# Ranks of queries and keys transposed by VectorE in 32x32 blocks and by transfers through device memory, with the queries' units amid the pool projection's

## The chip, the cores and the metric

One core of one Trainium2 chip runs the whole kernel in one launch. The metric is the device time of a launch in microseconds (us), the median of several executions. Nothing else runs on the chip.

## The reference, cut to what matters

Two layers of a decoder trunk on 256 tokens of width 1024, all in fp32. The mixer of a layer projects the normed tokens into several parts, among them the ranks `c_q` (384 wide) and `c_kv` (256 wide), each of which is normed and projected again; the pool branch has its own 512 columns `u_pool`:

```python
z = rms_norm(x, norm_pre) @ w_in
c_q, c_kv, k_r, u_conv, u_pool, gate_logits = jnp.split(z, split_at, axis=-1)
q = (rms_norm(c_q, q_norm) @ w_uq).reshape(B, S, N_HEADS, 96)      # 64 + 32 rotary
c_kv_n = rms_norm(c_kv, kv_norm)
k_nope, v = c_kv_n @ w_uk, c_kv_n @ w_uv
...                                  # causal attention, convolution, pooling, gates
x = x + rms_norm(merged @ w_mix_o, norm_post)
x = x + rms_norm((silu(h @ w_gate) * (h @ w_up)) @ w_down, ffn_norm_post)
```

## The kernel before, in words

The weights stream through the core in 135 units per layer, each 128 rows of up to 1024 fp32 numbers. A ring of 5 slots holds them. For every unit SyncE loads `raw` (line 398), ScalarE copies it into `w_hi`, rounded (`hi`, line 863), VectorE stores the rest as `w_lo` (`lo`, lines 1184 and 1188), and TensorE makes three products of high and low parts (`mm3`, lines 460 to 462). A slot is loaded again when `lo` of the unit five before is done (line 397); `hi` also waits until TensorE has used the slot; TensorE waits for `lo` (`unit_ready`). So each engine has one queue in program order, and the order of the work is written out by hand: the lists of `his`, `los` and `taps` in the scalar and vector blocks say after which unit something else stands.

The stage around the change, as it is before, in units of a layer: gate and value of the convolution (0 to 7), `CQ` (8 to 11, the rank of the queries), `CKV` (12 to 15, the rank of keys and values and the rotary key), `Q` (16 to 18, the queries out of their rank), `POOL` (19 to 22), `K` (23), `V` (24), and the 24 units of the gates (25 to 48), after each of which `attention(i)` puts a step of attention on TensorE's queue: scores, transposes of the probabilities, weighted values (lines 713 to 774).

A product needs the activation with its channels on the partitions. The ranks leave TensorE with tokens on the partitions, ScalarE scales them into `cq` (lines 955 and 968), and TensorE turns them with an identity (`transposes`, line 534): six for `CQ` before the third unit of `CKV`, four for `CKV` after `Q`. ScalarE copies the turned blocks out of PSUM as the high part (`hi_T`, line 897), VectorE stores the low part (`lo_T`, line 1216).

VectorE has one more task here: the convolution, 124 `taps` a layer (line 1263, 128x256 each), which are strewn between the `lo`s so that the last is done in the gates' stage; and it rotates and turns the heads of queries and keys with 32x32 transposes (`turn_heads`, line 1323), whose blocks are put in place by transfers on the POOL queue (line 1641) and on SyncE's (`move_keys`, line 360). In the gates' stage its loop (lines 1408 to 1427) has for gate unit i: `maxima` of the scores, `invert`, `divide`, `lo` of the unit four on, four taps. ScalarE's `exponentials` wait for `maxima`, TensorE's transposes of the probabilities (line 534, `tp<-const,qk`) for `exponentials`.

The hidden layer of the FFN is already turned in the other way: VectorE transposes 32x32 blocks (line 1502), SyncE moves the blocks from partition group to partition group inside SBUF (`place`, line 425, four issues at a time between loads), ScalarE and VectorE make high and low parts of what has landed (lines 1104 and 1509).

Of the kernel before, what the change touches and what calls it, by code (L numbers as in the profile page):

```python
# [14 lines left out]
P = 128  # L15
# [22 lines left out]
(U_G, U_A, U_CQ, U_CKV, U_Q, U_POOL, U_K, U_V, U_GATE, U_POOLO, U_ATTNO, U_CONVO, U_MIX, U_FFN,  # L38
 U_LAST, U_DOWN, UNITS) = (0, 4, 8, 12, 16, 19, 23, 24, 25, 49, 53, 57, 61, 69, 109, 113, 135)
# [19 lines left out]
def lo_count(g):  # L59
# [33 lines left out]
TP = (["X0", "X1", "X2", "X3", "HC0", "HC1", "CQ0", "CQ1", "CKV0", "CKV1",  # L93
# [44 lines left out]
def unit_scales(u):  # L138

    if U_Q <= u < U_POOL:  # L140
        return [(0, HEADS * QK, C_QN + u - U_Q)]
    if u in (U_K, U_V):
        return [(0, 512, C_KVN), (512, WU, C_KVN + 1)]
    if U_POOLO <= u < U_ATTNO:
        i = (u - U_POOLO) % 2
        return [(0, 512, C_PS + 2 * i), (512, WU, C_PS + 2 * i + 1)]
    return None


def build(nc, W, pool_w, par_d, const_d, gain_d, x_d, xc_d, pos_d, out_d):  # L150
    with ExitStack() as ctx:
# [59 lines left out]
        placed_q = [qk_flat[:, 512 * i:512 * (i + 1)] for i in range(QUADS - 1)] + [gates[:, 1, 512:1024]]  # L211
        rope_a, rope_b = hc[:, 0, :], hc[:, 1, :]
# [66 lines left out]
        k_nope = sem("k_nope")  # L279
        q_turned = sem("q_turned")  # L280
# [22 lines left out]
        stored = sem("stored")  # L303

# [48 lines left out]
        def move_keys(eng, l, part):  # L353

            for h in range(2):
                eng.wait_ge(misc_full[h], l * 2 + 1)
            for i in range(HEAD_MOVES // 2 * part, HEAD_MOVES // 2 * (part + 1)):
                c, q = divmod(i, QUADS)
                eng.wait_ge(k_turned, l * (QK // BLK) + c + 1)
                eng.dma_start(u_hc[BLK * c:BLK * (c + 1), q // 2, q % 2, :], turned_k[c][BLK * q:BLK * (q + 1), :]  # L360
                              ).then_inc(k_in[part], 16)

# [21 lines left out]
        def _(sp):  # L384
# [41 lines left out]

            for l in range(LAYERS):
                for u in range(0 if l else 1, UNITS):
# [10 lines left out]
                    if u == U_POOL:  # L439
                        load_pool_weights(l)  # L440
                    if u == U_GATE + 5:
                        move_keys(sp, l, 1)
# [14 lines left out]
        def _(pe):  # L457
# [23 lines left out]
            for l in range(LAYERS):  # L481
# [25 lines left out]
                def col_group(u0, n, per, width, pair, use, srcT, kt0=0, beside=None, after=None, mid=None, begun=0):  # L507

                    for i in range(begun, n):
# [143 lines left out]
                def cq_transposes(i):  # L653
                    if i == 2:
                        for t in range(TOK):
                            acc_freed(pe, l, t, "CQ")
                            transposes(TPN["CQ0"] + t, [(cq[:, t, c * P:(c + 1) * P], P) for c in range(3)])

                col_group(U_CKV, 4, 2, CKV_W, 1, "CKV", XT, beside=cq_transposes)

                for i in range(3):
                    unit_ready(U_Q + i)
                    for t in range(TOK):
                        if i == 0:
                            tp_emptied(pe, l, TPN["CQ0"] + t)
                            bank_free(t, "Q")
                            misc_wait(t, M_Q)
                        mm = tok_mm(base + U_Q + i, t, [i], 384, [acc[:, t, 0:384], misc[:, t, 0:384]], HT, 0, 2)
                        if t == 1:
                            mm.then_inc(unit_used, 1)  # L670
                        elif i == 2:
                            mm.then_inc(full[0], 1)
                for t in range(TOK):
                    acc_freed(pe, l, 2 + t, "CKV")
                    transposes(TPN["CKV0"] + t, [(cq[:, t, c * P:(c + 1) * P], P) for c in range(3, 5)])

                col_group(U_POOL, 4, 2, 512, 1, "POOL", XT)

                for t in range(TOK):
                    tp_emptied(pe, l, TPN["CKV0"] + t)  # L680
# [166 lines left out]
        def _(act):  # L847
# [3 lines left out]
            for l in range(LAYERS):  # L851
# [111 lines left out]
                for t in range(TOK):  # L963
                    hi_T(f"CQ{t}", hT_hi[:, H_CQ:H_CQ + 3, tokens(t)])
# [5 lines left out]
                his(20, 22)  # L970
# [3 lines left out]
                for t in range(TOK):  # L974
                    hi_T(f"CKV{t}", hT_hi[:, H_CKV:H_CKV + 2, tokens(t)])
# [7 lines left out]
                his(22, 23)  # L983
# [8 lines left out]
                his(23, 26)  # L992
# [156 lines left out]
        def _(dve):  # L1149
# [23 lines left out]
            for l in range(LAYERS):  # L1173
# [122 lines left out]
                for u in range(13, 16):  # L1296
                    lo(u)
                    taps(2)
                los(16, 17)
                for t in range(TOK):  # L1300
                    lo_T(f"CQ{t}", hT_lo[:, H_CQ:H_CQ + 3, tokens(t)], hT_hi[:, H_CQ:H_CQ + 3, tokens(t)])
                los(17, 18)
                taps(1)
                for u in range(18, 22):
                    lo(u)
                    taps(2)
                for t in range(TOK):
                    lo_T(f"CKV{t}", hT_lo[:, H_CKV:H_CKV + 2, tokens(t)], hT_hi[:, H_CKV:H_CKV + 2, tokens(t)])
                taps(3)
                los(22, 23)  # L1310
                taps(2)
# [14 lines left out]
                los(23, 24)  # L1326
                dve.wait_ge(q_roped, l + 1)
                turn_heads(q_sb, turned_q, q_turned)
                los(24, 25)
# [356 lines left out]
def unit_width(u):  # L1686
# [3 lines left out]
    if U_CKV <= u < U_Q:  # L1690
        return 2 * CKV_W
    if U_Q <= u < U_POOL:
# [4 lines left out]
def weight_stream(a):  # L1697
# [16 lines left out]
    put(U_POOL, pool, 2)  # L1714
# [73 lines left out]
```

## Time and profile before

| | us |
|---|---|
| median of 3 runs | 786.53 (786.52 to 786.84) |
| profiled execution, its own time | 786.49 |
| its span in the profile | 784.7 |
| PE busy | 776.2 (99%) |
| DVE busy | 573.3 (73%) |
| ACT busy | 421.8 (54%) |
| mean rate of the DMA engines | 197 GB/s |

The span runs from the first to the last recorded instruction; the execution's own time has 1.8 us more around it. PE is TensorE, DVE is VectorE, ACT is ScalarE, SP is SyncE; PEld is the loading of TensorE's stationary operand. The granted clock of TensorE has 9 or more tenths in every slice of the page, and its mean over the profiled execution is 0.998. The first layer's stage from `CKV` to the last gate unit runs from 40 to 154 us, the second layer's from 426 to 540 us. Durations of neighbouring instructions of one engine overlap a little, so that a start-to-start distance is shorter than a duration.

### The profile page before, as it was taken

What the parts mean: (1) busy time and instruction counts of PE and PEld (TensorE: products, weight loads), DVE (VectorE), ACT (ScalarE), POOL (GpSimd) and SP (SyncE); (2) the same over time, 40 slices, a digit from 0 to 9 for tenths busy, and PEclk for the clock granted to TensorE, in tenths of its full rate; (3) what the DMA queues carried; (4) which work ended last, traced back from release to release, by engine and by line L of the source; (5) the groups of instructions that cost most, each with busy time, mean ns of one, the idle gap of its engine ahead of it and who ended that gap; (6) DMA issues with size and microseconds to landing.
All of it is one profiled execution on the core that took longest, in us unless ns stands there. A gap on an engine that the chain in (4) does not pass through costs nothing.

```text
span 784.7 us, 10199 instructions
## 1 busy us (share of the span) xinstructions
PE 776.2 (99%) x3708; PEld 655.8 (84%) x3708; DVE 573.3 (73%) x826; ACT 421.8 (54%) x596; POOL 96.9 (12%) x147
## 2 busy tenths in 40 slices
PE   8999999999999999999999999999999999999997
PEld 7898888888888888888889988888888888888885
DVE  6689999889675666654476999996887665556553
ACT  6577455564554454454475666565546544445441
POOL 1624000122300000000121230002304000000000
PEclk9999999999999999999999999999999999999999
DMA  9677544545566666676464684444564666666731
GB/s 357 229 251 215 183 159 153 177 150 182 180 231 225 206 215 213 203 257 208 132 203 152 237 243 158 161 162 161 166 224 147 245 211 216 213 217 211 227 137 53
DMA packets 53456, 154.39 MB, mean 197 GB/s; under 512 B 10544, under 2 KB 15664, under 8 KB 53408
## 3 DMA queue, kind: packets, MB, share of 16 engines
q1 hardware_dynamic: 51856, 149.72, 57.5%
q0 software_dynamic: 1408, 3.52, 1.7%
q8 instruction: 29, 0.48, 0.2%
q10 hardware_dynamic: 144, 0.52, 0.2%
q14 instruction: 19, 0.16, 0.1%
HBM read 143.77 MB, written 1.05 MB: 185 GB/s over the span
## 4 chain that ended last, share of the span: by engine, by line
PE 98%; DMA 1%; ACT 0%; DVE 0%; issue 0%; DVEq 0%; POOLq 0%; SPq 0%; POOL 0%; ACTq 0%
PE acc L460 28%; PE acc L462 28%; PE acc L461 28%; PE acc L579 7%; PE tp L534 2%; PE misc L727 1%; PE tp L745 1%; PE tp L546 1%; DMA gates<-x_cols 1%; PE tp L709 0%; PE misc L462 0%; PE misc L461 0%; PE misc L460 0%; PE misc L694 0%; PE misc L696 0%; ACT w_hi L863 0%
## 5 line engine op out<-in xcount | busy, mean ns | idle before, releaser
L1188 DVE TENSOR_TENSOR w_lo<-raw,w_hi 128x1024 fp32r<-128x1024 f32 (+2 forms) x246 | 298.6, 1226 | 121.1 <-ACT w_hi L863 120.4
L863 ACT ACTIVATE w_hi<-raw 128x1024 fp32r<-128x1024 f32 (+2 forms) x252 | 257.9, 1039 | 162.8 <-PE acc L462 154.8
L460 PE MATMUL acc<-w_hi,xT_hi 128*128 128x512 f32 (+2 forms) x692 | 267.9, 387 | 0.0
L462 PE MATMUL acc<-w_hi,xT_lo 128*128 128x512 f32 (+2 forms) x692 | 264.9, 383 | 0.0
L461 PE MATMUL acc<-w_lo,xT_hi 128*128 128x512 f32 (+2 forms) x692 | 264.6, 382 | 0.0
L462 PEld LDWEIGHTS acc<-w_hi,xT_lo 128*128 128x128 f32 x692 | 129.9, 188 | 24.8
L461 PEld LDWEIGHTS acc<-w_lo,xT_hi 128*128 128x128 f32 x692 | 130.0, 188 | 24.0
L460 PEld LDWEIGHTS acc<-w_hi,xT_hi 128*128 128x128 f32 x692 | 130.0, 188 | 23.9
L460 PE MATMUL acc<-w_hi,hT_hi 128*128 128x512 f32 (+1 forms) x300 | 117.1, 390 | 0.0
L462 PE MATMUL acc<-w_hi,hT_lo 128*128 128x512 f32 (+1 forms) x300 | 116.2, 387 | 0.0
L461 PE MATMUL acc<-w_lo,hT_hi 128*128 128x512 f32 (+1 forms) x300 | 116.1, 387 | 0.0
L1263 DVE SCALAR_TENSOR_TENSOR cacc<-hcT,par,cacc 128x256 f32<-128x256 f32 x240 | 101.1, 480 | 0.0
L462 PEld LDWEIGHTS acc<-w_hi,hT_lo 128*128 128x128 f32 x300 | 56.3, 188 | 11.4
L461 PEld LDWEIGHTS acc<-w_lo,hT_hi 128*128 128x128 f32 x300 | 56.3, 188 | 11.0
L460 PEld LDWEIGHTS acc<-w_hi,hT_hi 128*128 128x128 f32 x300 | 56.3, 188 | 11.0
L1592 POOL TENSOR_SCALAR mean<-ssq 128x1 f32<-128x1 f32 x23 | 10.6, 462 | 442.6 <-ACT qk L882 442.0
L1052 ACT ACTIVATE qk<-misc,nmx 128x128 f32<-128x128 f32 (+1 forms) x32 | 13.2, 416 | 46.4 <-DVE nmx L1389 46.4
L1509 DVE TENSOR_TENSOR hT_lo<-gates,hT_hi 128x512 fp32r<-128x512 f32 (+1 forms) x24 | 14.4, 639 | 22.1 <-ACT hT_hi L1104 22.1
L1184 DVE SCALAR_TENSOR_TENSOR w_lo<-raw,par,w_hi 128x512 fp32r<-128x512 f32 (+1 forms) x30 | 25.7, 888 | 5.9 <-ACT w_hi L863 5.8
L1164 DVE TENSOR_TENSOR acc<-acc,gain 128x512 f32<-128x512 f32 x16 | 10.4, 692 | 25.6 <-ACT qk L882 22.6
L1104 ACT ACTIVATE hT_hi<-gates 128x512 fp32r<-128x512 f32 (+1 forms) x24 | 13.0, 587 | 26.8 <-DMA gates<-gates 26.8
L579 PE MATMUL acc<-w_hi,xT_hi 128*128 128x512 f32 x76 | 23.9, 396 | 1.0 <-ACT w_hi L863 1.0
(148 smaller groups left out, 639.0 us busy)
## 6 DMA issues: line engine op xcount, KB each, us to landing
raw<-weights SPq DMA_DIRECT2D x247, 512.0 KB, 3.7
raw<-weights SPq DMA_DIRECT2D x14, 384.0 KB, 3.5
gates<-gates SPq DMA_DIRECT2D x160, 32.0 KB, 2.5
raw<-weights SPq DMA_DIRECT2D x8, 288.0 KB, 4.1
gain<-gains SPq DMA_DIRECT2D x4, 512.0 KB, 6.8
qk<-gates POOLq DMA_DIRECT2D x18, 64.0 KB, 3.5
x_sb<-x_rows SPq DMA_DIRECT2D x2, 512.0 KB, 9.5
out_rows<-x_sb SPq DMA_DIRECT2D x4, 256.0 KB, 2.0
```

Source lines behind the costliest of these rows:

```text
L460: pe.matmul(out, a_hi, b_hi, start=start, stop=False)
L461: pe.matmul(out, a_hi, b_lo, start=False, stop=False)
L462: return pe.matmul(out, a_lo, b_hi, start=False, stop=stop)
L534: mm = pe.transpose(tp[0:rows, b, i * P:(i + 1) * P], src, ident)
L579: mm = pe.matmul(b, src[:, kt, tokens(t)], w[:, s, 512 * j:512 * (j + 1)], start=kt == 0 and src is xT_hi and w is w_hi, stop=last and kt ...
L863: ins = act.activation(w_hi[:, s, first:end], raw[:, s, first:end], ACT.Copy, scale=by)
L1052: e = act.activation(probs[:, n % 2, i, 0:keys], misc[:, n % 2, i * keys:(i + 1) * keys], ACT.Exp, bias=nmx[:, n % 2, i:i + 1], accum_out= ...
L1104: act.activation(hid_part(hT_hi, j, t), placed_for(j, t), ACT.Copy).then_inc(hid_hi, 1)
L1184: ins = dve.scalar_tensor_tensor(out=w_lo[:, s, first:end], in0=raw[:, s, first:end], scalar=par[:, l, col:col + 1], in1=f(w_hi[:, s, firs ...
L1188: ins = dve.tensor_tensor(w_lo[:, s, 0:width], raw[:, s, 0:width], f(w_hi[:, s, 0:width]), ALU.subtract)
L1263: ins = dve.scalar_tensor_tensor(out=cacc[:, c, :], in0=src, scalar=w, in1=cacc[:, c, :], op0=ALU.mult, op1=ALU.add)
L1509: dve.tensor_tensor(hid_part(hT_lo, j, t), placed_for(j, t), f(hid_part(hT_hi, j, t)), ALU.subtract).then_inc(hid_lo, 1)
```

## The change

The ten transposes of the ranks leave TensorE. VectorE transposes the ranks in 32x32 blocks (`turn_ranks`, four instructions a layer), SyncE writes the turned blocks to an array in device memory (`blocks_out`, one transfer a rank) and reads them back to their partitions (`blocks_in`, four transfers a rank, after a wait for the write), ScalarE and VectorE make high and low parts of them out of SBUF (`hi_ranks`, `lo_ranks`). The first two units of `POOL` now stand ahead of `Q` and the last two behind it. The pool weights are loaded two units later in the list. The places of `his`, `los` and `taps` are written anew: 44 taps instead of 45 stand ahead of the gates' loop.

```diff
@@ -35,8 +35,8 @@
 RING = 5
-(U_G, U_A, U_CQ, U_CKV, U_Q, U_POOL, U_K, U_V, U_GATE, U_POOLO, U_ATTNO, U_CONVO, U_MIX, U_FFN,
- U_LAST, U_DOWN, UNITS) = (0, 4, 8, 12, 16, 19, 23, 24, 25, 49, 53, 57, 61, 69, 109, 113, 135)
+(U_G, U_A, U_CQ, U_CKV, U_POOL, U_Q, U_POOL2, U_K, U_V, U_GATE, U_POOLO, U_ATTNO, U_CONVO, U_MIX, U_FFN,
+ U_LAST, U_DOWN, UNITS) = (0, 4, 8, 12, 16, 18, 21, 23, 24, 25, 49, 53, 57, 61, 69, 109, 113, 135)
 CKV_W = KV_RANK + ROPE
@@ -70,7 +70,7 @@
 LAST_UNIT = (
-    {"G": 3, "CQ": 11, "Q": 18, "K": 23, "GATE0": 28, "GATE2": 36, "GATE4": 44, "POOLO": 50, "ATTNO": 54,
+    {"G": 3, "CQ": 11, "Q": 20, "K": 23, "GATE0": 28, "GATE2": 36, "GATE4": 44, "POOLO": 50, "ATTNO": 54,
      "CONVO": 58, "MIX": 68, "F0": 72, "F1": 80, "F2": 88, "F3": 96, "F4": 104, "FL": 112, "DOWN": 134},
@@ -209,6 +209,10 @@
+        turned_r = gates[:, 0, 0:TOK * Q_RANK], u_sb[:, 0, :]
+        placed_r = gates[:, 1, 0:TOK * Q_RANK], u_sb[:, 1, :]
         rope_a, rope_b = hc[:, 0, :], hc[:, 1, :]
@@ -302,6 +311,11 @@
+        RANKS = ((H_CQ, Q_RANK // P, 0), (H_CKV, KV_RANK // P, Q_RANK))
+        between_r = [nc.dram_tensor(f"between_r{n}", (QUADS, P, TOK * tiles * BLK), F32, kind="Internal").ap()
+                     for n, (_, tiles, _) in enumerate(RANKS)]
@@ -359,6 +373,16 @@
+        def r_blocks(buf, n):
+            return buf.rearrange("p (q t k j) -> p q t k j", q=QUADS, t=TOK, k=RANKS[n][1])
...
+        def r_placed(n, t):
+            return r_blocks(placed_r[n], n)[:, :, t, :, :].rearrange("p q k j -> p k q j")
...
+        def r_part(dst, n, t):
+            first, tiles, _ = RANKS[n]
+            return dst[:, first:first + tiles, tokens(t)].rearrange("p k (q j) -> p k q j", q=QUADS)
@@ -423,6 +447,19 @@
+            def blocks_out(l, n):
...
+                sp.wait_ge(r_turned, TOK * (2 * l + n + 1))
+                sp.dma_start(between_r[n].rearrange("q p m -> p q m"),
+                             turned_r[n].rearrange("p (q m) -> p q m", q=QUADS)).then_inc(r_out, 16)
...
+            def blocks_in(l, n):
...
+                sp.wait_ge(r_out, 16 * (2 * l + n + 1))
+                for q in range(QUADS):
+                    sp.dma_start(placed_r[n][BLK * q:BLK * (q + 1), :].rearrange("f (a m) -> f a m", a=QUADS),
+                                 between_r[n][q].rearrange("(a f) m -> f a m", a=QUADS)).then_inc(r_in, 16)
@@ -436,8 +473,13 @@
                             sp.dma_start(x[:, t, :], x_d[t * P:(t + 1) * P, :]).then_inc(x_in[t], 16)
-                    if u == U_POOL:
+                    if u == U_POOL2:
                         load_pool_weights(l)
+                    for n, after in enumerate((U_Q + 1, U_POOL2 + 1)):
+                        if u == after:
+                            blocks_out(l, n)
+                        if u == after + 1:
+                            blocks_in(l, n)
                     if u == U_GATE + 5:
@@ -504,9 +546,10 @@
-                def col_group(u0, n, per, width, pair, use, srcT, kt0=0, beside=None, after=None, mid=None, begun=0):
...
-                    for i in range(begun, n):
+                def col_group(u0, n, per, width, pair, use, srcT, kt0=0, beside=None, after=None, mid=None, begun=0,
+                              ended=None):
...
+                    for i in range(begun, ended or n):
                         if beside:
@@ -650,19 +693,14 @@
-                def cq_transposes(i):
-                    if i == 2:
-                        for t in range(TOK):
-                            acc_freed(pe, l, t, "CQ")
-                            transposes(TPN["CQ0"] + t, [(cq[:, t, c * P:(c + 1) * P], P) for c in range(3)])
...
-                col_group(U_CKV, 4, 2, CKV_W, 1, "CKV", XT, beside=cq_transposes)
+                col_group(U_CKV, 4, 2, CKV_W, 1, "CKV", XT)
+                col_group(U_POOL, 4, 2, 512, 1, "POOL", XT, ended=2)
...
                         if i == 0:
-                            tp_emptied(pe, l, TPN["CQ0"] + t)
+                            pe.wait_ge(r_lo, TOK * 2 * l + t + 1)
                             bank_free(t, "Q")
@@ -670,14 +708,11 @@
                             mm.then_inc(full[0], 1)
-                for t in range(TOK):
-                    acc_freed(pe, l, 2 + t, "CKV")
-                    transposes(TPN["CKV0"] + t, [(cq[:, t, c * P:(c + 1) * P], P) for c in range(3, 5)])
...
-                col_group(U_POOL, 4, 2, 512, 1, "POOL", XT)
...
-                for t in range(TOK):
-                    tp_emptied(pe, l, TPN["CKV0"] + t)
...
+                col_group(U_POOL2 - 2, 4, 2, 512, 1, "POOL", XT, begun=2)
...
+                pe.wait_ge(r_lo, TOK * 2 * (l + 1))
                 col_group(U_K, 1, 2, 512, 0, "K", HT, kt0=H_CKV)
@@ -960,19 +995,25 @@
                     square(R_CQ + t, cq[:, t, 0:Q_RANK])
-                for t in range(TOK):
-                    hi_T(f"CQ{t}", hT_hi[:, H_CQ:H_CQ + 3, tokens(t)])
                 his(17, 20)
...
                                    scale=rstd(l, R_X + t)).then_inc(free[2 + t], 1)
-                his(20, 22)
+                his(20, 21)
                 for t in range(TOK):
...
                     square(R_CKV + t, cq[:, t, Q_RANK:Q_RANK + KV_RANK])
-                for t in range(TOK):
-                    hi_T(f"CKV{t}", hT_hi[:, H_CKV:H_CKV + 2, tokens(t)])
...
+                def hi_ranks(n):
...
+                    act.wait_ge(r_in, 16 * QUADS * (2 * l + n + 1))
+                    for t in range(TOK):
+                        act.activation(r_part(hT_hi, n, t), r_placed(n, t), ACT.Copy).then_inc(r_hi, 1)
...
+                hi_ranks(0)
+                his(21, 23)
+                hi_ranks(1)
                 if l == 0:
@@ -980,7 +1021,7 @@
                     act.preload_act_table(ACT.Tanh)
-                his(22, 23)
+                his(23, 25)
@@ -989,7 +1030,8 @@
                                        scale=stat(R_CQ + t)).then_inc(done[t], 1)
-                his(23, 26)
+                his(25, 26)
+                act.wait_ge(r_lo, TOK * 2 * (l + 1))
                 for t in range(TOK):
@@ -1293,22 +1335,46 @@
                 taps(3)
-                for u in range(13, 16):
...
+                def turn_ranks(n):
...
+                    _, tiles, at = RANKS[n]
+                    for t in range(TOK):
+                        acc_freed(dve, l, 2 * n + t, ("CQ", "CKV")[n])
+                        dve.transpose(r_blocks(turned_r[n], n)[:, :, t, :, :].rearrange("p q k j -> p k q j"),
+                                      cq[:, t, at:at + tiles * P].rearrange("p (k q j) -> p k q j", k=tiles, q=QUADS)
+                                      ).then_inc(r_turned, 1)
...
+                def lo_ranks(n):
...
+                    for t in range(TOK):
+                        dve.wait_ge(r_hi, TOK * (2 * l + n) + t + 1)
+                        dve.tensor_tensor(r_part(hT_lo, n, t), r_placed(n, t), f(r_part(hT_hi, n, t)),
+                                          ALU.subtract).then_inc(r_lo, 1)
...
+                for u in range(13, 15):
                     lo(u)
                     taps(2)
-                los(16, 17)
-                for t in range(TOK):
-                    lo_T(f"CQ{t}", hT_lo[:, H_CQ:H_CQ + 3, tokens(t)], hT_hi[:, H_CQ:H_CQ + 3, tokens(t)])
-                los(17, 18)
+                turn_ranks(0)
+                lo(15)
+                taps(2)
+                los(16, 18)
                 taps(1)
-                for u in range(18, 22):
-                    lo(u)
-                    taps(2)
-                for t in range(TOK):
-                    lo_T(f"CKV{t}", hT_lo[:, H_CKV:H_CKV + 2, tokens(t)], hT_hi[:, H_CKV:H_CKV + 2, tokens(t)])
+                lo(18)
+                taps(1)
+                turn_ranks(1)
+                lo(19)
+                taps(1)
+                lo_ranks(0)
+                lo(20)
+                taps(1)
+                lo(21)
+                taps(5)
+                lo_ranks(1)
+                lo(22)
                 taps(3)
-                los(22, 23)
-                taps(2)
+                los(23, 25)
+                taps(1)
                 if l == 0:
@@ -1323,10 +1389,8 @@
-                los(23, 24)
                 dve.wait_ge(q_roped, l + 1)
                 turn_heads(q_sb, turned_q, q_turned)
-                los(24, 25)
                 for t in range(TOK):
@@ -1711,7 +1775,8 @@
     put(U_CKV, c_kv, 2)
-    put(U_POOL, pool, 2)
+    put(U_POOL, pool[:, :D // 2], 2)
+    put(U_POOL2, pool[:, D // 2:], 2)
     put(U_Q, a["w_uq"], 1)
```

The rest of the diff declares the semaphores `r_turned`, `r_out`, `r_in`, `r_hi` and `r_lo`, takes the four names out of the list of PSUM transposes, and lets the tests of unit numbers go by the new places.

## Rows read from the trace of the kernel before

**Rows 1.** The page, part 4: the chain that ended last, by engine.

```profile
PE 98%; DMA 1%; ACT 0%; DVE 0%; issue 0%; DVEq 0%; POOLq 0%; SPq 0%; POOL 0%; ACTq 0%
```

**Rows 2.** Two stretches: length, busy PE, PEld, DVE, ACT, POOL, clock, DMA, GB/s.

```profile
57.20:95.00 37.80, 37.80 (x184) 31.79 (x182) 37.37 (x71) 23.93 (x41) 8.94 (x18) 1.00 0.64 196
443.00:481.00 38.00, 38.00 (x186) 32.10 (x185) 37.63 (x72) 23.28 (x41) 8.90 (x18) 1.00 0.65 194
```

**Rows 3.** The chain in order of time (start us, us): rank transposes.

```profile
43.37 0.66 PE tp L534 x6
53.47 0.44 PE tp L534 x4
...
429.71 0.66 PE tp L534 x6
```

**Rows 4.** Timeline, second scores, first layer: start us, us, engine, line, operation.

```profile
93.84 0.69 DVE L1389 TENSOR_REDUCE nmx<-misc 128x2 f32<-128x512 f32 x1
...
95.39 0.20 ACT L1052 ACTIVATION_READ_ACCUMULATOR qk<-misc,nmx 128x1 f32 x1
...
95.64 0.65 PE L534 MATMUL tp<-const,qk 128*128 128x128 f32 x4 [0.58 <-ACT qk L1052]
```

**Rows 5.** Timeline, the same instructions in the second layer.

```profile
480.57 0.20 ACT L1052 ACTIVATION_READ_ACCUMULATOR qk<-misc,nmx 128x1 f32 x1
...
481.01 0.25 PEld L534 LDWEIGHTS tp<-const,qk 128*128 128x128 f32 x2
```

**Rows 6.** VectorE's waits, 37 to 97 us, first layer: us, times, longest.

```profile
DVE hT_lo L1216 <- ACT hT_hi L897: 1.2, 2, 0.9
DVE w_lo L1188 <- ACT w_hi L863: 1.0, 1, 1.0
DVE w_lo L1184 <- ACT w_hi L863: 0.2, 1, 0.2
```

**Rows 7.** Timeline of VectorE, second layer: its two longest waits in brackets.

```profile
430.60 1.02 DVE L1216 TENSOR_TENSOR hT_lo<-tp,hT_hi 128x384 fp32r<-128x384 f32 x2 [0.98 <-ACT hT_hi L897]
...
473.06 1.29 DVE L1216 TENSOR_TENSOR hT_lo<-tp,hT_hi 128x512 fp32r<-128x512 f32 x2 [0.23 <-ACT hT_hi L897]
```

**Rows 8.** Groups by line and form: count, busy us, mean ns, idle before.

```profile
L1502 DVE STREAM_TRANSPOSE gates<-u_hc 128x512 f32<-128x512 f32 x20 | 13.0, 686 | 0.0
...
L1502 DVE STREAM_TRANSPOSE gates<-u_hc 128x256 f32<-128x256 f32 x4 | 1.5, 421 | 0.0
L1509 DVE TENSOR_TENSOR hT_lo<-gates,hT_hi 128x256 fp32r<-128x256 f32 x4 | 1.5, 418 | 0.0
```

**Rows 9.** Timeline of VectorE, first layer, 40 to 79 us.

```profile
40.84 0.76 DVE L1188 TENSOR_TENSOR w_lo<-raw,w_hi 128x576 fp32r<-128x576 f32 x1
...
45.46 1.02 DVE L1184 SCALAR_TENSOR_TENSOR w_lo<-raw,par,w_hi 128x768 fp32r<-128x768 f32 x1 [0.18 <-ACT w_hi L863]
...
75.09 2.06 DVE L1263 SCALAR_TENSOR_TENSOR cacc<-hcT,par,cacc 128x256 f32<-128x256 f32 x5
77.08 1.22 DVE L1188 TENSOR_TENSOR w_lo<-raw,w_hi 128x1024 fp32r<-128x1024 f32 x1
```

**Rows 10.** Timeline of ScalarE, first layer, a table load.

```profile
54.87 1.28 ACT L982 ACT_TABLE_LOAD   x1
```

**Rows 11.** DMA view, 38 to 56 us.

```profile
DMA packets 1508, 5.03 MB, mean 279 GB/s; under 512 B 160, under 2 KB 160, under 8 KB 1505
```

**Rows 12.** DMA view, loads issued at 41.6 and 58.5 us: KB, us to landing.

```profile
raw<-weights SPq DMA_DIRECT2D x1, 512.0 KB, 5.9
...
raw<-weights SPq DMA_DIRECT2D x1, 512.0 KB, 3.2
```

**Rows 13.** DMA view: one `place` of the FFN at 262 us; output stores.

```profile
gates<-gates SPq DMA_DIRECT2D x4, 32.0 KB, 2.5
...
out_rows<-x_sb SPq DMA_DIRECT2D x2, 256.0 KB, 2.0
```

**Rows 14.** Timeline of SyncE: the issues of that `place`.

```profile
262.29 2.41 SPq L425 DMA_DIRECT2D gates<-gates  x4
```

More of the change, by code:

```diff
@@ L89, in fulls @@
     return len([u for u in upto if pair == 0 or u not in WIDE])
-TP = (["X0", "X1", "X2", "X3", "HC0", "HC1", "CQ0", "CQ1", "CKV0", "CKV1",
+TP = (["X0", "X1", "X2", "X3", "HC0", "HC1",
        "MT0", "MT1", *(f"{piece}{n}" for n in range(8) for piece in "PV"), "O0", "O1",
@@ L138, in unit_scales @@
 def unit_scales(u):
-    if U_Q <= u < U_POOL:
+    if U_Q <= u < U_POOL2:
         return [(0, HEADS * QK, C_QN + u - U_Q)]
@@ L279, in build @@
         k_nope = sem("k_nope")
+        r_turned = sem("r_turned")
+        r_out = sem("r_out")
+        r_in = sem("r_in")
+        r_hi = sem("r_hi")
+        r_lo = sem("r_lo")
         q_turned = sem("q_turned")
@@ L1689, in unit_width @@
         return 2 * Q_RANK
-    if U_CKV <= u < U_Q:
+    if U_CKV <= u < U_POOL:
         return 2 * CKV_W
-    if U_Q <= u < U_POOL:
+    if U_Q <= u < U_POOL2:
         return HEADS * QK
```

## The prediction

> **What bounds the kernel now.** I read the chain first: TensorE makes 98% of the path to the end [rows 1], so an edit is worth what it does to TensorE's queue, and work on another engine is free until TensorE waits for it. The reader is to see next, in the stretches by engine, that VectorE isn't far behind in just this stage: from 57 to 95 us it is busy 37.37 of 37.80 us, in the second layer 37.63 of 38.00 [rows 2]. The third view says where the two meet. In the first layer VectorE ends the `maxima` of the second scores at 94.53 (93.84 plus 0.69), ScalarE's exponentials end at 95.59, and TensorE, idle for 0.58 us, starts the transposes at 95.64 with that wait noted beside it [rows 4]. In the second layer exponentials end at 480.77 and TensorE comes for them at 481.01 [rows 5]: 0.25 us of slack. So at this one place, in both layers, TensorE already goes by VectorE's clock, and everything that VectorE does before it, back to its last idle moment, is on the path. Its idle time ahead of it, from the start of the stage on, is 2.4 us in the first layer [rows 6] and 1.4 in the second, where the wait of 1.0 us for `w_hi` is missing and the others are 0.98, 0.23 [rows 7] and, as in the first, 0.2; that is all that new work may use up.
>
> **What the change removes.** Ten 128x128 transposes a layer: 0.66 us for the six of `CQ` and 0.44 for the four of `CKV` [rows 3], 1.10 a layer, 2.2 in all. That gain is only kept if TensorE isn't held later in the layer. TensorE's products are the same otherwise; their new order costs it nothing by itself. ScalarE and VectorE copy as many columns as before, out of SBUF instead of PSUM, at the same price (a 256-wide low part takes 418 ns out of SBUF [rows 8]). One tap less ahead of the gates' loop gives VectorE 0.40 us back (five taps take 1.99 us from start to start [rows 9]); it is done at the end of the loop, where I cost it at nothing: the place that binds lies before it.
>
> **What it adds to VectorE.** Four block transposes a layer. 512 wide they take 686 ns, 256 wide 421 [rows 8]; 384 between them is 553. Less the 0.07 us by which neighbours overlap, two of 384 and two of 256 are 0.96 + 0.70 = 1.66 us a layer. Nothing hides it: from here to the second scores VectorE has no idle time beyond the 2.4 and 1.4 us.
>
> **What it adds in waits.** VectorE now waits in its own queue for blocks that go out to memory and come back (`lo_ranks`), and behind that wait stand the low parts of units 20 to 24, the rotation and all later taps. I walk the first layer by its clock; the second has the same distances.
>
> - `turn_ranks(0)` stands where `lo(15)` began, at 40.84 [rows 9], and is done at 41.8. VectorE then has `lo` of units 15 (0.7), 16 and 17 (1.14 each [rows 9]), 18 and 19 (0.94 each by the 1.02 us row [rows 9] less its overlap), five taps (2.0) and `turn_ranks(1)` (0.7): it is at `lo_ranks(0)` at 49.3.
> - The write, 393 KB, stands behind loads in SyncE's transfers, which drain at 279 GB/s here [rows 11]. No row shows a write to memory from amid loads. Its bounds are 2.0 us, the landing of an output store with nothing ahead of it, and 5.9, the load that had most ahead of it [rows 12, 13]. I take 3.4, near the 3.2 of a load with a free queue [rows 12], since only one or two loads are ahead: landed at 45.2.
> - SyncE issues the four reads in 2.41 us as it does a `place` [rows 14], the last 1.8 after the first, and they land 2.5 later [rows 13]: 49.5. With 0.5 for ScalarE's copy VectorE goes on at 50.0. **First wait 0.7 us.** (ScalarE is done with its squares at 49.2, so even an early landing saves little.) TensorE wants this rank at 51.8, so it isn't held here.
> - VectorE does `lo_ranks(0)` (0.96), units 20 and 21 (2.1) and six taps (2.4) and is at `lo_ranks(1)` at 55.4.
> - SyncE, held since 43 by its wait and the four issues, is free at 47.6. It issues the loads of units 21 and 22 and the pool weights, which are moved to this place, and only then the second write, at 49. Ahead of it on the transfers lie 1.31 MB, with its own 0.26 MB 1.57 MB; from 49.5 on at 0.3 MB a us that is landed at about 54.3 (the rate taken a little above the mean, as nothing comes in between). Last read issued 1.8 later, landed 2.5 later: 58.6; copied 59.0. **Second wait 3.6 us.** Bounds: none, if each transfer lands at 2.0 us (the reads at 54.8), and 8 if each takes 5.9.
> - In the first layer ScalarE must then load a table (1.28 us [rows 10]) before units 23 and 24 and the copies of the queries for which the rotation waits; before, this lay in VectorE's 1.0 us wait. I estimate that this costs 0.8 us more.
>
> Work that leans on SyncE's queue, the loads of units 20 to 26, comes up to 8 us later than before. It is costed at nothing, as `hi` of unit 23 now runs no earlier than 60; without that cover each us would stop ScalarE. The head transfers of POOL and SyncE start about 4 us later with VectorE and are needed at the first scores, which are late as well.
>
> **The sum.** VectorE's lateness at the second scores. First layer: 1.66 - 0.40 - 2.4 + 0.7 + 3.6 + 0.8 = +3.96. Second: 1.66 - 0.40 - 1.4 + 0.7 + 3.6 - 0.25 of slack = +3.91. TensorE arrives 1.10 early and stands until then: for `lo` of units 25 and 26 already, then for the exponentials. The 2.2 us saved are inside this wait, not to be taken off again. Nothing gives it back, for TensorE is full to the end. The profiled execution's span goes from 784.7 to 792.6, its own time from 786.49 to 794.4; the median before, 786.53, is the same within 0.1, so 794.4.
>
> **Rivals.**
>
> *The blocks are back in time.* Both waits vanish: first layer 1.66 - 0.40 - 2.4 = -1.1, second -0.1, with the slack -0.4. Then 785.1 to 785.5, not measurably slower. For it: VectorE has 7.6 us of work between turning the queries' rank and needing it, and a free queue would bring the second rank at 54.8, ahead of 55.4. Against: the queue isn't free, 279 GB/s over this stretch [rows 11]. It decides at a landing of the second reads at 55. Chance 0.14.
>
> *TensorE keeps its gain.* It would have the 2.2 us and the 0.58 us of waiting: 786.5 - 2.8 = 783.7, faster. The mechanism: VectorE gains 0.6 us or more at the second scores, because its transposes or taps pack tighter than rows 8 and 9 say, and the blocks are in time too. For it: TensorE's gain is the only certain term. Against: even without waits VectorE falls behind by 0.1 us in the second layer. Chance 0.10.
>
> *The write is slow to be acknowledged.* If a write amid loads lands at 5.9 instead of 3.4 us, each of the two costs 2.5 us more, 5 a layer: 804. TensorE would stand at the first `Q` product too. For it, nothing in the trace: stores land in 2.0 us [rows 13], though with a free queue. Chance 0.10. The Trainium skill ("DMA: Bandwidth & Descriptors", "Anatomy of one DMA" and "Latency and other measured facts") says that most of a transfer's fixed 2 us is the receipt of the last write, heaviest for device memory and growing with its load. By that rule the write lands late here; the row of the stores agrees with the 2 us and shows nothing of the growth.
>
> The same skill ("VectorE: DVE Perf Modes", "The three transpose paths" and its rules) gives a full 128x128 transpose to TensorE, since VectorE's blocks don't cross 32 partitions. The trace bears it out as a price: 0.11 us of TensorE a tile against 0.17 of VectorE and two transfers.
>
> **The numbers.** The forecast has 0.66, for any second wait between 1 and 6 us, with times from 788 to 799. 0.2% (1.6 us) is about what a measurement of this kernel can tell from no change. Faster 0.10, within 0.2% 0.14, slower 0.76. The range takes the forecast's bounds and a part of the case of blocks in time: 786.5 to 799.5.
>
> **What would show it.** Right: no L534 on `gates`; four rank transposes a layer on VectorE near 0.55 and 0.42 us; VectorE idle before `lo_ranks(1)` for 3 to 4 us, released by ScalarE's `hi_ranks`, and that by the reads; TensorE idle in the order of 1 us before the first gate units and at the second scores' transposes, with ACT as the releaser; after 100 us the same intervals as before, shifted. Wrong: VectorE's idle time before `lo_ranks` under 1 us, or TensorE with no waits between 60 and 96 us though VectorE came late, which would mean that the place I call binding isn't.

## The result, and the profile after

The changed kernel takes 795.15 us (median of 4 runs, 794.76 to 795.66), the one before 786.52 on the same chip: a ratio of 1.0107, with a 95% interval of 1.0095 to 1.0119, 8.6 us slower. The profiled execution's own time is 795.66, its span 793.5: 2.16 us lie around the span, where the kernel before has 1.8. It is so in every run (2.1 to 2.2 us in all kernels with the change, 1.8 to 1.9 in the two without it), so 0.3 us of the loss lie outside what the profile records, and their cause stays open. I read the profile in the order of the prediction. First the page: the span, the busy engines, the memory traffic and the chain that ended last.

```profile
span 793.5 us, 10179 instructions
...
PE 776.1 (98%) x3688; PEld 652.1 (82%) x3688; DVE 577.9 (73%) x834; ACT 422.2 (53%) x596; POOL 96.3 (12%) x147
...
HBM read 145.08 MB, written 2.36 MB: 186 GB/s over the span
...
PE 83%; DVE 9%; DMA 4%; ACT 1%; SPq 1%; issue 1%; DVEq 0%; POOLq 0%; ACTq 0%; POOL 0%
PE acc L502 24%; PE acc L504 24%; PE acc L503 24%; PE acc L622 7%; DVE cacc L1305 3%; DVE w_lo L1230 2%; DMA between_r<-u_hc 2%; PE tp L577 2%; PE tp L780 1%; DMA between_r<-gates 1%; PE misc L762 1%; DVE gates L1389 1%; SPq L461 1%; PE tp L589 1%; DMA gates<-x_cols 1%
```

TensorE is as busy as before, but no longer alone on the chain, where it had 98% [rows 1]: VectorE and transfers now have 13 points of it (1 before), and the two writes to device memory (`between_r<-u_hc`, `between_r<-gates`) stand there by name.

Next the timeline of VectorE in the first layer, for [rows 9], and its waits from 37 to 99 us, for [rows 6].

```profile
41.18 1.04 DVE L1344 STREAM_TRANSPOSE gates<-gates 128x384 f32<-128x384 f32 x2
...
47.55 0.77 DVE L1344 STREAM_TRANSPOSE u_hc<-gates 128x256 f32<-128x256 f32 x2
...
50.91 1.03 DVE L1352 TENSOR_TENSOR hT_lo<-gates,hT_hi 128x384 fp32r<-128x384 f32 x2 [1.29 <-ACT hT_hi L1012]
...
54.48 2.06 DVE L1305 SCALAR_TENSOR_TENSOR cacc<-hcT,par,cacc 128x256 f32<-128x256 f32 x5
60.23 0.76 DVE L1352 TENSOR_TENSOR hT_lo<-u_hc,hT_hi 128x256 fp32r<-128x256 f32 x2 [3.68 <-ACT hT_hi L1012]
...
63.67 2.74 DVE L1226 SCALAR_TENSOR_TENSOR w_lo<-raw,par,w_hi 128x512 fp32r<-128x512 f32 x4 [0.35 <-ACT w_hi L898]
```

```profile
DVE hT_lo L1352 <- ACT hT_hi L1012: 5.0, 2, 3.7
DVE w_lo L1226 <- ACT w_hi L898: 0.4, 1, 0.4
DVE hT_lo L1258 <- ACT hT_hi L932: 0.2, 1, 0.2
```

Both waits of `lo_ranks` (line 1352) are there. The releaser named is ScalarE's copy; ScalarE's own timeline says what that waited for, the reads:

```profile
50.36 0.94 ACT L1012 ACTIVATE hT_hi<-gates 128x384 fp32r<-128x384 f32 x2 [0.89 <-DMA gates<-between_r]
...
59.78 0.73 ACT L1012 ACTIVATE hT_hi<-u_hc 128x256 fp32r<-128x256 f32 x2 [3.10 <-DMA u_hc<-between_r]
```

And SyncE's timeline with the DMA view (38 to 60 us; KB, median us to landing) splits each way into write and reads.

```profile
42.25 0.38 SPq L454 DMA_DIRECT2D between_r<-gates  x1
...
46.65 1.75 SPq L461 DMA_DIRECT2D gates<-between_r  x4
...
49.87 0.43 SPq L454 DMA_DIRECT2D between_r<-u_hc  x1
...
56.37 1.75 SPq L461 DMA_DIRECT2D u_hc<-between_r  x4
```

```profile
between_r<-gates SPq DMA_DIRECT2D x1, 384.0 KB, 4.4
gates<-between_r SPq DMA_DIRECT2D x4, 96.0 KB, 2.1
...
between_r<-u_hc SPq DMA_DIRECT2D x1, 256.0 KB, 6.5
u_hc<-between_r SPq DMA_DIRECT2D x4, 64.0 KB, 2.0
```

The smaller write takes longer, 6.5 us against 4.4, because two loads of 512 KB and the pool weights (256 KB) were issued in the 1.4 us before it (x2 and x3 test this). The reads, with almost nothing ahead of them, land in 2 us.

Last, TensorE in the first layer, all stretches from 60 to 101 us in which it stood still (in brackets us and releaser); where there was one such row before [rows 4], there are now seven.

```profile
62.18 0.50 PE L502 MATMUL acc<-w_hi,xT_hi 128*128 128x512 f32 x1 [0.27 <-DVE w_lo L1230]
...
65.47 0.47 PE L502 MATMUL acc<-w_hi,hT_hi 128*128 128x512 f32 x1 [0.25 <-ACT qk L1031]
...
68.94 0.46 PE L729 MATMUL misc<-const,u_hc 128*128 128x130 f32 x2 [0.48 <-issue]
...
74.30 0.50 PE L502 MATMUL acc<-w_hi,xT_hi 128*128 128x512 f32 x1 [0.56 <-DVE w_lo L1230]
...
78.41 0.50 PE L502 MATMUL acc<-w_hi,xT_hi 128*128 128x512 f32 x1 [1.09 <-DVE w_lo L1230]
...
93.82 0.41 PE L577 MATMUL tp<-const,qk 128*128 128x128 f32 x2 [1.14 <-DVE hT_lo L1258]
...
100.75 0.66 PE L577 MATMUL tp<-const,qk 128*128 128x128 f32 x4 [0.58 <-ACT qk L1094]
```

The second scores' transposes start at 100.75 instead of 95.64, 5.11 late, of which 0.34 was there before the stage began. From there to the end of the layer the lateness stays at 5.1 us. In the second layer it grows once more in the same stage, from 5.00 to 8.84. I measure all kernels in this way below: by how much TensorE's first product of the same unit starts later than in the trace of before, as growth within a layer. For this change it is **+4.8 and +3.8 us**.

The bracketed idle time understates a stop, since ends of matmuls are modelled: where the bracket says 0.58 [rows 4], removing the wait gave 0.80 (below).

### The profile page after: what moved, and what is told of

It is laid out like the page before. It is cut to its first block, busy times and chain, and to the rows that moved or that the text cites. A ratio compares the mean times of both kernels' runs of the same rounds, so it can differ in the third digit from the quotient of the medians.

```text
span 793.5 us, 10179 instructions
## 1 busy us (share of the span) xinstructions
PE 776.1 (98%) x3688; PEld 652.1 (82%) x3688; DVE 577.9 (73%) x834; ACT 422.2 (53%) x596; POOL 96.3 (12%) x147
## 4 chain that ended last, share of the span: by engine, by line
PE 83%; DVE 9%; DMA 4%; ACT 1%; SPq 1%; issue 1%; DVEq 0%; POOLq 0%; ACTq 0%; POOL 0%
PE acc L502 24%; PE acc L504 24%; PE acc L503 24%; PE acc L622 7%; DVE cacc L1305 3%; DVE w_lo L1230 2%; DMA between_r<-u_hc 2%; PE tp L577 2%; PE tp L780 1%; DMA between_r<-gates 1%; PE misc L762 1%; DVE gates L1389 1%; SPq L461 1%; PE tp L589 1%; DMA gates<-x_cols 1%
## 5 line engine op out<-in xcount | busy, mean ns | idle before, releaser
L1656 POOL TENSOR_SCALAR mean<-ssq 128x1 f32<-128x1 f32 x23 | 8.1, 352 | 435.7 <-ACT qk L917 435.2
```

## The experiments

My theory: TensorE stands for VectorE, and VectorE for the blocks' way through memory. Rivals: the change in VectorE's own work, the new order of the units, or the displaced loads.

**x1: no transfers.** `hi_ranks` takes the turned blocks where VectorE wrote them; the transfers are left out. Left out of the computation: the placing of the blocks across partition groups.

```diff
 def r_placed(n, t):
-    return r_blocks(placed_r[n], n)...
+    return r_blocks(turned_r[n], n)...
...
-for n, after in enumerate((U_Q + 1, U_POOL2 + 1)):
...
 def hi_ranks(n):
-    act.wait_ge(r_in, 16 * QUADS * (2 * l + n + 1))
+    act.wait_ge(r_turned, TOK * (2 * l + n + 1))
```

> The changed kernel without the ten transfers of the ranks: ScalarE waits for VectorE's turned blocks and both copy straight out of them. What it leaves out is the placing of the blocks, so that the queries, keys and values come from wrongly placed ranks. Theory (the loss is VectorE's wait for the blocks on their way): VectorE's waits at lo_ranks fall from 5.0 us to about 0.5 in the first layer and from 3.8 to 0 in the second, and the time to 786.5 to 787.5, the time before the change. Rival A (the block transposes and the new order cost it by themselves): the time stays above 791. Rival B (TensorE's order, the queries' units amid the pool's, costs it): TensorE still waits for more than 2 us between 60 and 100 us.

785.88 us, 0.9991 [0.9982, 1.0]. That is 0.6 under the expected range. The whole loss is gone with the transfers, and VectorE waits nowhere at `lo_ranks`. Growth -1.0 and 0.0: without the transfers the change is worth next to nothing, although ten transposes a layer have left TensorE. (Since SyncE isn't held either, the loads are earlier too; x1 alone doesn't tell the blocks' own way from the loads that it displaces.) That needed an explanation of its own (x7).

**x2: the second write right behind the first reads**, ahead of load 21; the pool weights stay.

```diff
-for n, after in enumerate((U_Q + 1, U_POOL2 + 1)):
-    if u == after:
-        blocks_out(l, n)
-    if u == after + 1:
-        blocks_in(l, n)
+if u == U_Q + 1:
+    blocks_out(l, 0)
+if u == U_Q + 2:
+    blocks_in(l, 0)
+    blocks_out(l, 1)
+if u == U_POOL2 + 1:
+    blocks_in(l, 1)
```

> The changed kernel with the second write issued directly behind the first reads, ahead of the loads of units 21 and 22 and the pool weights; its reads stay behind the load of unit 22. Theory (the second rank is late because 1.3 MB of loads are ahead of its write in SyncE's queue): the second reads land at about 56.3 us instead of 59.8, VectorE's wait at lo_ranks(1) falls from 3.7 to about 0.3 us, and the time by 3.4 a layer, to 788 to 789. Rival (memory itself is slow, the write and its acknowledgement, wherever they stand): the wait falls by under 1 us and the time stays above 793.

792.81 us, 1.0084 [1.0069, 1.0099]: 2.3 us back where 6 to 7 were expected. The DMA view (38 to 60 us) shows that the write is quicker and the reads are slower:

```profile
between_r<-u_hc SPq DMA_DIRECT2D x1, 256.0 KB, 2.6
...
u_hc<-between_r SPq DMA_DIRECT2D x4, 64.0 KB, 4.8
```

The write lands in 2.6 us instead of 6.5, but now the reads stand behind the loads of units 21 and 22 and the pool weights, and take 4.8 instead of 2.0. So the time is no property of the write: it is whatever SyncE issued ahead, in whichever of the two steps. Yet that is the smaller part of the miss. VectorE's timeline shows the greater:

```profile
54.28 1.22 DVE L1232 TENSOR_TENSOR w_lo<-raw,w_hi 128x1024 fp32r<-128x1024 f32 x1 [1.81 <-ACT w_hi L900]
...
57.88 0.76 DVE L1354 TENSOR_TENSOR hT_lo<-u_hc,hT_hi 128x256 fp32r<-128x256 f32 x2 [0.40 <-ACT hT_hi L1014]
```

At `lo_ranks(1)` the first layer waits 0.40 us instead of 3.68, as the theory said (0.3). But VectorE now stands 1.81 us for the high part of unit 21, whose load is behind the write and lands 5.0 us after its issue (3.8 in the change). In the change ScalarE had that high part at 53.31 and VectorE took it at 53.34, so there was nothing to spare. In the second layer both waits are there, 1.97 us for unit 21 and 1.64 at `lo_ranks(1)`. The growth is +3.0 and +3.7: in the second layer the edit gains almost nothing. The displaced loads, one of the rivals above, are thus a limit right behind the blocks' way, and a cure has to serve both.

**x3: the pool weights later**, at `U_GATE` instead of `U_POOL2`; nothing else.

> The changed kernel with the pool weights (256 KB) loaded at the first gate unit instead of ahead of the second write. Theory (bytes ahead of the write in the queue, at 0.3 MB a us): the second wait is 0.8 to 0.9 us shorter in each layer and the time 793.3 to 793.6. Rival (only the number of transfers or SyncE's waiting counts): no change, 795.

793.19 us, 1.0085 [1.007, 1.01]: 2.0 us back. VectorE's longer wait goes from 3.7 to 2.7 in the first layer. In the second it goes from 3.8 to 2.1, but a wait of 0.8 for a unit's high part comes up. In all, 256 KB ahead of the write cost 1 us a layer.

**x9: both.** Load 21 goes while write 0 is under way, ahead of reads 0 and write 1; reads 1 follow after a single load; pool weights at `U_GATE`.

```diff
-                    if u == U_POOL2:
+                    if u == U_GATE:
                         load_pool_weights(l)
...
+                    if u == U_Q + 1:
+                        blocks_out(l, 0)
+                    if u == U_POOL2:
+                        blocks_in(l, 0)
+                        blocks_out(l, 1)
+                    if u == U_POOL2 + 1:
+                        blocks_in(l, 1)
```

> The changed kernel with SyncE's order such that each rank transfer has as little as possible ahead of it: the load of unit 21 goes while the first write is under way, the second write follows the first reads, its reads come behind the load of unit 22, the pool weights at the first gate unit. Theory (the waits are places in line, of the write and of the reads alike): the first wait stays at 1 to 1.5 us, as three round trips' fixed parts are in it, the second falls from 3.7 to under 0.5, and the time to 787.5 to 789. Rival (the round trip itself sets the second wait): above 791.

789.7 us (788.78 to 790.07, 6 runs), 1.0035 [1.0023, 1.0047], 0.7 above what was expected. The order of SyncE's issues alone was worth 5.4 of the 8.6 us. VectorE's waits at `lo_ranks(1)` and for unit 21 are both gone; which of the two is worth how much, this run doesn't separate. What is left of the blocks' way is one wait, the first (from 37 to 99 us; 1.1 in the second layer):

```profile
DVE hT_lo L1354 <- ACT hT_hi L1014: 1.7, 1, 1.7
```

**x5: the ten transfers issued by GpSimd**, so that they wait in no line with the loads and hold none back.

> The changed kernel with the ten transfers of the ranks issued from GpSimd's queue instead of SyncE's; nothing else moved. SyncE is then not held, and the transfers are no longer in line behind the loads but share the engines with them. Theory (the waits are a place in line, not the round trip): VectorE's second wait is under 1.5 us instead of 3.7, and the time 787 to 790. Rival (the DMA engines are full in this stretch, so that it doesn't matter which queue the bytes are in): the wait stays over 3 us and the time over 793.

809.1 us, 1.0286 [1.026, 1.0312]: 14 us worse than the change, and the opposite of what I expected. DMA view (38 to 62 us), VectorE's wait and TensorE's:

```profile
between_r<-gates POOLq DMA_DIRECT2D x1, 384.0 KB, 5.5
gates<-between_r POOLq DMA_DIRECT2D x4, 96.0 KB, 6.9
...
between_r<-u_hc POOLq DMA_DIRECT2D x1, 256.0 KB, 6.0
u_hc<-between_r POOLq DMA_DIRECT2D x4, 64.0 KB, 2.2
```

```profile
58.63 1.03 DVE L1334 TENSOR_TENSOR hT_lo<-gates,hT_hi 128x384 fp32r<-128x384 f32 x2 [8.67 <-ACT hT_hi L994]
```

```profile
59.29 0.66 PE L484 MATMUL acc<-w_hi,hT_hi 128*128 128x384 f32 x1 [6.07 <-issue]
```

SyncE's waits in the change had a use that I had overlooked: while SyncE waits for the write it issues no loads, so the reads find idle transfers and land in 2.1 us. Here the loads run on, and the same reads take 6.9. The way by GpSimd isn't slow by itself: the second rank's reads, issued at 58.88 when almost nothing else was being moved, landed in 2.2. (GpSimd's norms now stand between its transfers, so that the second write goes out at 52.63 instead of 49.87; VectorE's second wait is 0.8 nonetheless.) TensorE stands 6.1 us ahead of the first product of `Q`, for which the prediction's third rival had the place, though not the cause. The Trainium skill ("DMA: Bandwidth & Descriptors", "Issuing engines are not separate DMA queues") says that transfers started by different engines run on the same 16 DMA engines and interleave, and that only the time of issuing is saved; this trace agrees with the sharing.

**x4: 12 taps later**, from ahead of the gates' loop into its steps from the seventh on, so that VectorE makes up its lateness (4.8 us of work) before the scores.

```diff
-                taps(3)
+                taps(1)
...
-                taps(3)
+                taps(1)
...
-                    taps(5)
+                    taps(1)
...
-                    taps(4)
+                    taps(5 if i >= 6 else 4)
```

> The changed kernel with 12 of the 44 taps moved from ahead of the gates' loop to its steps 6 and later (five a step instead of four); the waits for the blocks stay. Theory (the end is set where TensorE goes by VectorE's clock, at the low parts of units 25 and 26 and at the second scores): VectorE is 4.8 us earlier at the second scores, TensorE doesn't wait there, only the waits at units 22 to 26 stay, some 2 us a layer, and the time is 789 to 791. Rival (TensorE is held by the blocks' late landing itself, at the products out of the ranks): the taps change nothing, 795.

795.43 us, 1.0115 [1.0098, 1.0131], nothing gained. In the second layer it did what was expected (+2.0 instead of +3.8), in the first it did harm (+6.0). The low parts of units 28 to 30 were now done earlier, which let SyncE issue six loads in a row from 77.9 us on. GpSimd's last two head transfers were issued behind the first of them; the last reached SBUF 5.7 us after its issue, at 84.19 (3.5 us in the change), and TensorE needed it:

```profile
84.28 1.19 PE L762 MATMUL misc<-u_hc,gates 96*128 96x128 f32 x4 [2.85 <-issue]
85.26 3.62 PE L744 MATMUL tp<-sg,pw_sb 128*128 128x256 f32 x8
```

The stretches of this kernel (length; busy PE, PEld, DVE, ACT, POOL; granted clock; DMA share; GB/s) show what followed:

```profile
84.00:86.00 2.00, 1.72 (x6) 1.66 (x7) 1.37 (x5) 0.04 (x1) 0.00 (x0) 0.50 1.02 414
86.00:88.00 2.00, 2.00 (x6) 1.55 (x6) 1.69 (x3) 1.38 (x5) 0.00 (x0) 0.50 0.67 274
88.00:90.00 2.00, 2.00 (x7) 1.53 (x6) 0.98 (x2) 1.08 (x2) 0.00 (x0) 0.50 0.69 254
90.00:92.00 2.00, 2.00 (x10) 1.68 (x9) 2.00 (x6) 1.15 (x2) 0.00 (x0) 0.94 0.06 25
```

After the 2.85 us without a matmul the granted clock is 0.50, that is 1.2 GHz instead of 2.4, for 6 us; unit 28 starts 6.2 us late where unit 27 was 1.2 late. Of the 6.0 us that TensorE is later by the end of the slow stretch, half is the stop and half the clock.

**x11: only 4 taps later**, `taps(5)` to `taps(3)`, and the loop as in x4.

> The changed kernel with four taps instead of twelve moved from ahead of the gates' loop behind its step 6; the blocks' waits stay. Theory (TensorE goes by VectorE's clock at the second scores, and twelve taps only failed because the loads that they let through crowded the head moves): 1.2 us earlier in the first layer and 1.6 in the second, 792 to 792.8. Rival (the second scores aren't what binds, TensorE waits for the head moves before them): unchanged, 795.

794.24 us, 1.0089 [1.0072, 1.0106]: 0.9 back where 2.4 to 3.2 were expected. The second scores did come 1.7 us earlier in the first layer (growth +3.1 there instead of +4.8). But the taps come back in the loop from the seventh step on, and there TensorE stopped anew, where neither the kernel before nor the change has a wait:

```profile
142.13 0.66 PE L577 MATMUL tp<-const,qk 128*128 128x128 f32 x4 [0.78 <-ACT qk L1094]
```

That gave 1.1 us back.

**x6: the kernel before with 12 taps later** (the edit of x4).

> The kernel before the change, with the 12 taps moved behind step 6 of the gates' loop, as in x4_taps_late. Theory (TensorE waits 0.58 us for VectorE at the second scores of the first layer and nowhere else): 785.9 to 786.5 if the head moves land in time. Rival (loads that VectorE frees earlier crowd the head moves, as in the run with late taps, and TensorE waits at the first scores and loses clock): 788 to 791.

785.64 us, 0.9989 [0.9979, 0.9999]: the fastest kernel of the study that computes everything, 0.9 us under before. The wait of [rows 4] is gone; TensorE gained 0.80 us at that place.

**x7: x1 with 4 taps later**, to see what TensorE's ten transposes a layer are worth when VectorE is in time everywhere. The placing of the blocks is left out as in x1.

> x1_no_transfer (no transfers of the ranks, wrongly placed blocks) with four taps moved from ahead of the gates' loop to its steps 6 and later. Theory (without the blocks' waits only VectorE's lateness at the second scores keeps TensorE from its 1.10 us a layer): TensorE keeps them and the 0.58 us, 783.6 to 784.2. Rival (removing the ten transposes is worth less than the chain of waits shows, as TensorE meets another wait): 785 to 786, as x1.

784.94 us, 0.9979 [0.997, 0.9989], about 1 us less gained than expected. Growth -1.5 and -0.5. Only one stop of TensorE in this stage has a bracket, and it is at a place where the kernel before has no wait, the first product of `POOL` right behind `CKV`:

```profile
47.06 0.47 PE L497 MATMUL acc<-w_hi,xT_hi 128*128 128x512 f32 x1 [0.28 <-ACT gates L996]
```

It waits for ScalarE to copy `CKV` out of the PSUM banks that `POOL` uses too. Before, the products of `Q` stood between the two. Start to start the step takes 0.57 us where 0.13 is usual, and in the second layer 0.26; the product behind it takes 0.08 more. So the new order costs some 0.55 us in the first layer, half of what the transposes save, and 0.26 in the second: up to the first scores TensorE keeps 0.52 and 0.84 of its 1.10 us, in x1 0.54 and 0.82. The rest of the growth is elsewhere. In the first layer it is -0.80 for the wait of [rows 4] and -0.13 at the first scores' transposes, where x6 gains the same. In the second it is +0.3 at the later scores' transposes (521.62), in front of which VectorE now has five taps a step. So the whole gain open to the change on TensorE was 1.4 us of 786.5, not 2.2.

**x8: x1 with every block transpose done twice**, the first time into a buffer that nobody reads; the placing is left out as in x1.

> x1_no_transfer with every block transpose of the ranks done a second time, into a buffer that nobody reads. Theory (each us of VectorE's work ahead of the second scores is a us of the end): 1.66 us more a layer, 3.3 in all, 789.0 to 789.4. Rival (VectorE's extra work is mostly hidden, and the transfers' traffic was the cost): under 787.

788.58 us, 1.0025 [1.0016, 1.0035], 0.4 under the expected range. VectorE has 1.66 us more a layer, and TensorE is 1.4 and 1.3 later than in x1: VectorE's work in this stage is paid at some 0.8 of its price.

**x10: x9 and taps moved**: three into VectorE's first wait, three more later.

```diff
-                taps(1)
+                taps(4)
                 lo_ranks(0)
...
-                    taps(5)
+                    taps(2)
...
-                    taps(4)
+                    taps(5 if i >= 6 else 4)
```

> x9_line_order with three taps put into VectorE's first wait and six fewer ahead of the gates' loop, so that three go to its steps 6 and later. Theory (a wait that VectorE fills with taps costs nothing, and taps behind the second scores are free): close to the kernels without transfers, 785 to 786.5, faster than the kernel before the change if at all by 0.1 to 0.2%. Rival (loads freed earlier crowd the head moves, as in x4): above 788.

787.54 us (786.08 to 788.77, 10 runs), 1.0009 [1.0, 1.0019], 1.0 above the expected range; the profiled execution (786.16) is one of the fastest. The change can so be brought back by 7.6 us, to the time of before but not below it. Its first layer shows what x11 did:

```profile
137.96 0.66 PE L579 MATMUL tp<-const,qk 128*128 128x128 f32 x4 [0.68 <-ACT qk L1096]
```

## Why the prediction was right, and where not

- **What binds.** Right, and shown: TensorE stood for the gates' first units and at the second scores, where the prediction placed it, and took up the old intervals after 101 us. Incomplete: there are also stops at the pool branch's products with the band (line 729, 0.48) and at the first scores' transposes, for the low parts of line 1258 (1.14), and x11 found one more place, the later scores at 142 us, where VectorE binds as soon as taps are moved there.
- **Removed and added work.** The four transposes take 558 and 424 ns (553 and 421 predicted). x8 shows that some 80% of their 1.66 us a layer are paid.
- **"their new order costs it nothing by itself."** This step failed: the new order costs TensorE some 0.55 us in the first layer and 0.26 in the second, at the first product of `POOL` (x7). It didn't show in the time, since TensorE stood later anyway; it did show in x1 and x7. The rival in which TensorE keeps its gain had 783.7; x7, with only this wait and 0.3 us at later scores left, has 784.94, of which 0.3 lie outside the span.
- **First wait.** Predicted 0.7 in each layer, measured 1.29 in the first and none in the second. The write took 4.4 us, not 3.4; SyncE issues four reads in 1.75 us, not 2.41, and they land in 2.1, not 2.5.
- **Second wait.** Predicted 3.6, measured 3.68 and 3.8. The write landed at 56.35, two us after the 54.3 predicted; VectorE came 1.1 later (56.5 instead of 55.4), and the reads were 1 us quicker. The size is right by errors that offset each other; the mechanism, the place behind loads and pool weights, is shown by x2, x3 and x9.
- **Table load.** Predicted 0.8, measured 0.35 as a wait of line 1226.
- **The sum.** Predicted +3.96 and +3.91, measured +4.8 and +3.8. From VectorE's waits (5.5 and 4.0 us against 2.4 and 1.4) and its work (+1.26) I get 4.4, and, less the slack, 3.6; some 0.3 us a layer lie in gaps that carry no releaser, and I leave them open. The 0.3 us outside the span had no term either. That 794.4 comes so near to 795.15 is in part luck: inside the second wait errors of 1 to 2 us cancel.
- **Loads late at no cost**: right for the change, but with nothing to spare at unit 21 (0.03 us), and in x2 it failed by 1.8 and 2.0 us of VectorE's time. x4 shows the other side, that loads made earlier can do harm.
- **Rivals.** The blocks back in time: x1 gives 785.88 for it, where 785.1 to 785.5 was worked out (its own terms, -1.1 and -0.4, give 785.0); the pool weights and the loads decided against it. The slow acknowledgement isn't what made the second write slow: it took 6.5 us, but 2.6 in x2, with loads behind it and none just ahead. The Trainium skill ("DMA: Bandwidth & Descriptors", "Latency and other measured facts") has the rule that the receipt of a write to device memory grows with that memory's load. No run here shows that growth by itself: in x5 the writes took 5.5 and 6.0 us beside running loads, which the sharing of the transfers explains as well.

## What to carry to other kernels

A transfer on a shared queue costs what has been issued ahead of it, so its place in the issuing order is worth more than its size, and a read back after a write needs a good place twice. What moves up in that order pushes something back: here a weight load that had nothing to spare (x2). Before work is taken off the bounding engine, ask which wait the moved order uncovers: a PSUM bank that two neighbouring groups share can eat half the gain, as in the first layer here. Work postponed out of one tight stretch has to be followed to where it lands, and so do the loads that it lets go earlier.

## What the runs showed of the hardware

- A pause of 2.85 us of TensorE (x4) was followed by 6 us at a granted clock of 0.50, and one of 6.07 us (x5) by a mean of 0.77 from 60 to 70 us. The change itself has a mean of 0.999; its longest pause, 2.49 us ahead of 8.84 us, was followed by no fall (1.00 from 8 to 16 us), and the longest in the stage above is 1.14.
- The first rank's reads (96 KB each) took 2.1 us on SyncE's queue with the loads held back and 6.9 on GpSimd's beside running loads; the second's (64 KB) took 2.0 with loads held back and 4.8 behind loads on the same queue.
